# Last expert tile: down weights loaded and used in five equal-width steps, the last narrow piece issued from ScalarE's queue

## What is computed

```
h = silu(ragged_dot(xs, w_gate, sizes)) * ragged_dot(xs, w_up, sizes)     # 2048 -> 512 per expert
y = ragged_dot(h, w_down, sizes)                                          # 512 -> 2048
y = y * gates_flat[order][:, None]
out = zeros_like(xt).at[token_of].add(y)
h = h + out
return rms_norm(h, final_norm_g)
```

## Time and profile before

| | us |
|---|---|
| median of 3 runs | 1982.48 |
| lowest and highest | 1981.11, 1984.16 |
| the profiled execution, its own time | 1982.84 |
| its span in the trace | 1980.0 |
| mean granted TensorE clock | 0.954 |

### The profile page before, as it was taken

One profiled execution on the slowest core, in us unless ns is written; L12 is line 12 of the kernel. 1 busy time (PEld: TensorE's weight loads), 2 busy tenths in 40 slices (PEclk: granted clock), 3 DMA queues, 4 the chain that ended last, 5 costly groups with the idle time before them and its releaser, 6 DMA issues.

```text
span 1980.0 us, 30734 instructions
## 1 busy us (share of the span) xinstructions
PE 1791.9 (91%) x12867; PEld 1139.0 (58%) x12867; DVE 788.3 (40%) x1516; ACT 248.2 (13%) x580; POOL 178.8 (9%) x204
## 2 busy tenths in 40 slices
PE   6999999999999989999355899999999999999666
PEld 4888999789997879999311233333333333333222
DVE  7666595277467544333400122221222222223015
ACT  3012111200325331000200000000000000000004
POOL 1453342000000000000100000000000000000000
PEclk9999999999999999999677899999999999999888
DMA  5343333321222232221699999999999999999996
GB/s 216 109 130 92 90 104 87 98 65 43 65 70 75 70 146 86 65 85 44 289 423 421 425 425 422 423 423 422 418 422 412 420 423 426 417 423 423 408 405 225
DMA packets 80393, 506.58 MB, mean 256 GB/s; under 512 B 18785, under 2 KB 23029, under 8 KB 46977
## 3 DMA queue, kind: packets, MB, share of 16 engines
q1 hardware_dynamic: 62706, 480.40, 60.4%
q0 software_dynamic: 5152, 15.81, 2.4%
q10 hardware_dynamic: 12400, 8.36, 1.7%
HBM read 498.32 MB, written 12.99 MB: 258 GB/s over the span
## 4 chain that ended last, share of the span: by engine, by line
PE 71%; DMA 20%; DVE 4%; issue 2%; ACT 1%; SPq 1%; ACTq 0%; DVEq 0%; POOL 0%; POOLq 0%
PE psum L958 20%; PE psum L1269 17%; PE psum L961 15%; DMA arena<-in_moe_w_gate 14%; PE psum L1233 6%; PE psum L1296 3%; DMA arena<-in_moe_w_up 3%; DMA arena<-in_moe_w_down 3%; PE psum L1116 2%; DVE arena L1704 2%; PE psum L1017 1%; PE psum L1363 1%; PE psum L1375 1%; DVE arena L1707 1%; DMA arena<-hs_rows,arena 1%
## 5 line engine op out<-in xcount | busy, mean ns | idle before, releaser
L1269 PE MATMUL psum<-arena 128*32 128x512 f32 x3584 | 423.1, 627 | 82.4 <-DMA arena<-in_moe_w_gate 34.6
L958 PE MATMUL psum<-arena 128*128 128x128 f32 x3584 | 412.6, 277 | 3.5 <-issue 3.5
L958 PEld LDWEIGHTS psum<-arena 128*128 128x128 f32 x3584 | 407.0, 193 | 10.9 <-issue 10.4
L1704 DVE TENSOR_TENSOR arena<-psum,arena 128x512 f32<-128x512 f32 (+1 forms) x319 | 211.7, 680 | 402.1 <-PE psum L1233 379.5
L1269 PEld LDWEIGHTS psum<-arena 128*32 128x32 f32 x3584 | 120.4, 115 | 378.0 <-issue 376.9
L961 PE MATMUL psum<-arena 128*128 128x256 f32 x1456 | 322.4, 380 | 1.1 <-DVE arena L1704 1.1
L961 PEld LDWEIGHTS psum<-arena 128*128 128x128 f32 x1456 | 273.4, 190 | 39.0 <-issue 2.1
L1704 DVE TENSOR_TENSOR arena<-arena,psum 128x256 f32<-128x256 f32 (+2 forms) x172 | 75.1, 437 | 473.0 <-PE psum L958 217.1
L1296 PE MATMUL psum<-arena 128*32 128x512 f32 x1664 | 185.9, 605 | 20.9 <-DMA arena<-in_moe_w_down 20.6
L1704 DVE TENSOR_TENSOR arena<-arena 128x240 f32<-128x240 f32 (+17 forms) x464 | 187.4, 446 | 33.0 <-ACT arena L1424 25.2
L1233 PE MATMUL psum<-arena 128*128 128x512 f32 x416 | 192.4, 605 | 0.0
(11 more groups left out here) (213 smaller groups left out, 993.0 us busy)
## 6 DMA issues: line engine op xcount, KB each, us to landing
arena<-in_moe_w_gate SPq DMA_DIRECT2D x64, 2048.0 KB, 28.0
arena<-in_moe_w_up SPq DMA_DIRECT2D x64, 2048.0 KB, 26.3
arena<-in_moe_w_down SPq DMA_DIRECT2D x60, 2048.0 KB, 27.9
arena<-in_w_in SPq DMA_DIRECT2D x86, 512.0 KB, 4.6
arena<-in_w_out SPq DMA_DIRECT2D x32, 512.0 KB, 4.6
arena<-in_x SPq DMA_DIRECT2D x8, 1024.0 KB, 8.3
hs_rows<-arena ACTq DMA_DIRECT2D x4, 1024.0 KB, 4.8
arena<-in_moe_w_down SPq DMA_DIRECT2D x4, 1024.0 KB, 15.2
```

The lines of the kernel that those rows point to most:

```text
L958: last = mm(B(bank, [(1, P)], off=t * P), F(a + t * P, P), F(w + i * P, P), start=start and t == 0, stop=(i == KH - 1), skip_group_check=True)
L1269: last = mm(B(bank, [(1, FE)], 32 * g, 32), F(XT + c * CAP + 32 * g, 32), F(SLOT[slot] + (c % 8) * FE, FE), start=(c == 0), stop=(c == KD ...
L1704: return v.tensor_tensor(o, a, b, op)
```

## The change

Pieces 0 and 1 are loaded apart, each with one load per expert of 512 columns (1 MB, rows of 2 KB). SP issues pieces 0 to 3 in order. The four loads of piece 4 leave SP's queue: ACT issues two of them between its silu and its copy of the hidden activations, and two between its copies of the gain and its copy of piece 0. It waits on `slot_used` of buffers 4 to 7 for them, and loads the four expert numbers into registers beforehand. PE works all five pieces product by combination. DVE takes them in the same order, and does two of the four `times_g` of piece 3 behind its copy of piece 4.

```diff
-        PIECES = ((0, 512, 16, 0, D // 2), (512, 512, 16, 512, D // 2), (1024, 512, 20, 0, 512), (1536, 256, 20, D, 256),
+        PIECES = ((0, 512, 16, 0, 512), (512, 512, 16, D, 512), (1024, 512, 20, 0, 512), (1536, 256, 20, D, 256),
                   (1792, 256, 20, D + 1024, 256))
@@ SP
-            for k in range(4):
-                slot, n = parts[16 + k]
-                sp.wait_ge(slot_used[slot], n + 1)
-                sp.dma_start(V(SLOT[slot], [(D // 2, FT2), (1, D // 2)]),
-                             down_columns(four[k], 0, D // 2)).then_inc(slot_in[slot], 16)
...
+            for p, (lo, cols, first, at_, row) in enumerate(PIECES[:LASTP]):
                 for k in range(4):
+                    slot, n = parts[first + k]
+                    dst = V(SLOT[slot] + at_, [(row, FT2), (1, cols)])
+                    if at_ == 0:
+                        sp.wait_ge(slot_used[slot], n + 1)
+                        sp.dma_start(dst, down_columns(four[k], lo, cols)).then_inc(slot_in[slot], 16)
+                    else:
+                        sp.dma_start(dst, down_columns(four[k], lo, cols)).then_inc(tail_in[p], 16)
@@ PE
-                y_part(0)
-                y_part(1)
-                combine_part(0)
-                combine_part(1)
-                for p in range(2, NPC):
+                for p in range(NPC):
                     y_part(p)
                     combine_part(p)
@@ ACT
                 A(F(SIL, FE), B(2, [(1, FE)]), ACT.Silu).then_inc(silu_done, 1)
+                if between is not None:
+                    between()
                 act.wait_ge(hT_full, n + 2)
...
+            four = [act.value_load(ORDV[0:1, bass.ds(NE - 4 + k, 1)], min_val=0, max_val=NE - 1) for k in range(4)]
+
+            def last_columns(ks):
+                lo, cols, first, at_, row = PIECES[LASTP]
+                for k in ks:
+                    slot, before = last_parts()[first + k]
+                    act.wait_ge(slot_used[slot], before + 1)
+                    act.dma_start(V(SLOT[slot] + at_, [(row, FT2), (1, cols)]),
+                                  down_columns(four[k], lo, cols)).then_inc(tail_in[LASTP], 16)
+
+            hidden_act(LAST, ends(last_parts())[0], lambda: last_columns((0, 1)))
...
+            last_columns((2, 3))
             y_copy_last(0)
@@ DVE
-            y_copy(1)
             dve.wait_ge(fg_done, 4)
-            for p in (0, 1):
...
+            for p in range(LASTP):
+                if not Y_ACT[p]:
+                    y_copy(p)
                 for t in range(TB):
                     add(t, p)
-            for p in (0, 1):
...
+                if p < LASTP - 1:
+                    for t in range(TB):
+                        times_g(t, p)
+            times_g(0, LASTP - 1)
+            times_g(1, LASTP - 1)
             y_copy(LASTP)
+            times_g(2, LASTP - 1)
+            times_g(3, LASTP - 1)
```

More of the change, by code:

```diff
@@ L512, in build @@
         fg_in, fg_spread, fg_done = sem("fg_in"), sem("fg_spread"), sem("fg_done")
-        tail_in = [sem("tail_in0"), sem("tail_in1")]
+        tail_in = [None, sem("tail_in1"), None, sem("tail_in3"), sem("tail_in4")]
         g_done, out_dve, out_act, out_done = (
@@ L619, in build, with down_columns @@
         wg_d, wu_d, wd_d = d["moe_w_gate"], d["moe_w_up"], d["moe_w_down"]
+        def down_columns(e, lo, n):
+            return wd_d[bass.ds(e, 1), :, lo:lo + n].rearrange("e (m p) n -> p (e m) n", p=P)
         block = ctx.enter_context(nc.Block())
@@ L653, in part @@
                 sp.dma_start(dst, half_of_expert(e, which, half)).then_inc(slot_in[slot], 16)
-            def down_columns(e, lo, n):
-                return wd_d[bass.ds(e, 1), :, lo:lo + n].rearrange("e (m p) n -> p (e m) n", p=P)
             def expert(i):
@@ L701, in _ @@
                 part(four[j % 4], parts[j], j // 8, j // 4 % 2)
-            for k in range(4):
-                slot, n = parts[16 + k]
-                sp.wait_ge(slot_used[slot], n + 1)
-                sp.dma_start(V(SLOT[slot], [(D // 2, FT2), (1, D // 2)]),
-                             down_columns(four[k], 0, D // 2)).then_inc(slot_in[slot], 16)
[L707 to L712, removed]
-                for k in range(4):
-                    slot = parts[20 + k][0]
-                    sp.dma_start(V(SLOT[slot] + at_, [(row, FT2), (1, n)]),
-                                 down_columns(four[k], lo, n)).then_inc(tail_in[i], 16)
+            for p, (lo, cols, first, at_, row) in enumerate(PIECES[:LASTP]):
+                for k in range(4):
+                    slot, n = parts[first + k]
[5 more added lines that the diff above has]
+                        sp.dma_start(dst, down_columns(four[k], lo, cols)).then_inc(tail_in[p], 16)
             for t in range(TB):
@@ L1353, in y_part @@
                     here = parts[first:first + 4]
-                    if p >= 3:
-                        pe.wait_ge(tail_in[p - 3], 4 * 16)
-                    elif p != 1:
+                    if at_:
+                        pe.wait_ge(tail_in[p], 4 * 16)
+                    else:
                         for slot, before in here:
@@ L1604, in _, with hidden_act @@
             A(F(RE2, TB), F(RDF, TB), ACT.Exp).then_inc(gates_exp, 1)
-            def hidden_act(n, gate_end):
+            def hidden_act(n, gate_end, between=None):
                 slot, before = gate_end
@@ L1638, in _ @@
                 act.wait_ge(o_added, NOV * 16 + 17)
-            hidden_act(LAST, ends(last_parts())[0])
+            four = [act.value_load(ORDV[0:1, bass.ds(NE - 4 + k, 1)], min_val=0, max_val=NE - 1) for k in range(4)]
[7 more added lines that the diff above has]
+            hidden_act(LAST, ends(last_parts())[0], lambda: last_columns((0, 1)))
             for q in range(4):
```

## The result

| | median, us | runs | ratio to before (95% interval) |
|---|---|---|---|
| before | 1982.35 | 22 | |
| changed | 1985.95 (1983.13 to 1989.31) | 22 | 1.0018 (1.0012 to 1.0024) |

The change costs 3.6 us, 0.18%: clear of zero, and just inside the 0.2% that the prediction took as the line (the interval reaches beyond that line). The profiled execution has a span of 1985.2 us, 5.2 us longer than the one of before, and was itself one of the longer ones (1987.65 us).

The account below looks back on a forecast made before the run. The landing at 1932.2 and PE's chain behind it set the end. Piece 2 starting 2.2 us late was the only term: 1982.48 + 2.2 = 1984.7 us; range 1981.0 to 1988.0, the forecast's own 1983.9 to 1985.4.

Parts of the forecast that it names:

- The gain at piece 0: On PE, piece 0's product starts 2.7 us sooner; after exposed copies PE is ready for piece 2 0.7 us sooner.
- The landing of piece 2: Piece 4's early loads go ahead of piece 2, which lands at 1950.3; PE starts its product 2.2 us later.
- The price of sharing, by whole loads: On the DMA engines, piece 2 lands after 12 loads of 1 MB plus all of piece 4, 5.95 to 7.4 us.
- ACT held at its issue: Rival: each ACT issue of piece 4 waits up to 4.9 us for SP's; 1986.9 or 1991.4 us; chance 0.14.
- The clock in the new wait: Rival: PE's clock falls while waiting for piece 2, its product takes 3.4 us more; 1988.1 us; chance 0.08.
- DVE's new order and the four register loads: DVE's gain products stay hidden, reordering piece 3's costs at worst 0.1 us; ACT's register loads fall in idle time, costing nothing.

Follow-up runs that it names:

- the old cut: The kernel before, with ACT issuing piece 4's loads; pieces 0 and 1 stay one load of 4 KB rows per expert: 1984.96 us, ratio 1.0012.

## Why the prediction was right or wrong

**The gain at piece 0: right.** Expected: start 1929.6, end of the product 1934.9, of the combination 1939.4, ready for piece 2 at 1947.5, 0.7 us sooner than before. Measured: 1929.74, 1934.7, 1939.04 and 1947.2. The copies stand open in the chain at 0.71 and 0.81 us. The kernel without ACT's loads agrees with the sum, 1.2 us below against the 0.7 forecast, but its interval includes no gain at all.

**The landing of piece 2: right, to 0.2 us partly by luck.** Expected 1950.3 and a start at 1950.4, 2.2 us late; measured 1950.5 and 1950.63, 2.4 us late. The 1950.3 was the middle of a range with no reason for it (6.7 us for piece 4), on top of 1943.6 for the rest; with piece 4 last on SP the rest landed at 1944.3, and 6.2 us separate that from the changed kernel. The reason held, since the same order of bytes on one queue gave the same loss, and a late second queue gave none. By the Trainium skill's rule on queues ("DMA: Bandwidth & Descriptors", section "Queues, rings and completion order") the engines take turns by packet; 901 packets against 901 in the old cut's trace agree.

**The price of sharing, by whole loads: right for piece 2, too simple elsewhere.** The prediction charged piece 2 with all of piece 4. That is right, since all of piece 4 is through by 1942.2. The expectation for the old cut charged pieces 0 and 1 in the same way, and that was twice too much (2.1 us, not 4 to 5): only part of ACT's rows had their turn by then, which explains some of it, and the rest is open. Piece 1 landed in time in the changed kernel (PE took it at 1939.04 without a wait), so that nothing of the forecast hung on this.

**ACT held at its issue: a rival, refuted.** ACT's four issues took 0.38 to 0.42 us. The last two (0.94 us for both, from 1929.19) stand within an issue of SP's that lasted 7.22 us. First that SP issue, then ACT's last:

```profile
L708 SPq DMA_DIRECT2D arena<-in_moe_w_down x1: 7220/7220/7220, 1927.6 to 1927.6; - x1
...
L1638 ACTq DMA_DIRECT2D arena<-in_moe_w_down x1: 383/383/383, 1929.7 to 1929.7; - x1
```

Had ACT's issue had to wait for the end of SP's, it would have ended after 1934.8. The Trainium skill ("Perfetto Trace Analysis", section "DMA Instruction — HWDGE (DVE, Sync)") says that an issue holds a lock on the shared descriptor generator until its descriptors are made. In this trace SP cannot have held such a lock for the whole of its issue; what SP was waiting for in it, no run shows. The chance of 0.14 rested on this rival, and the upper part of the range on it and on the clock.

**The clock in the new wait: the step that was mis-sized.** The sum held nothing for it. It was put as a rival beside the forecast with a chance of 0.08 and a price of 3.4 us. Both traces of the changed kernel show it, at 2.8 and 1.3 us, on top of the late landing: it is a consequence of the wait, and belonged in the sum with the chance that the wait gives it. The price was that of a product done wholly at the low level; in both traces the clock came back before the end. The wait was also longer than the 2 to 3 us that the rival was weighed with (3.44), since PE came 0.3 us sooner and the data 0.2 us later. The result lies 1.25 us above the forecast and 0.55 us above the forecast's own range, though inside the whole one. The loss is 3.6 us where 2.2 was forecast, and the clock is the only term the runs show that is large enough for the difference; its exact part of the median is not shown.

**DVE's new order and the four register loads: nil, as expected.** The copy of piece 1 starts at 1942.75, with the products of the gain done at 1942.25 (DVE rows of after):

```profile
1939.76 2.49 DVE L1707 TENSOR_TENSOR arena<-arena 128x512 f32<-128x512 f32 x4
1942.75 0.69 DVE L2386 COPY arena<-psum 128x512 f32<-128x512 f32 x1 [0.50 <-PE psum L1357]
```

The half microsecond of idleness between them says that DVE waited for PE, not PE for DVE. The first add of piece 4 begins 0.8 us after PE's last combination starts, before and after the change (1963.97 in the earlier trace rows, the combination at 1963.17).

## What to carry to other kernels

A load on a second queue is not behind the first queue's backlog: it takes its turns at once, row for row. Give a second queue only what is needed next, or issue it late. When an edit opens a wait on PE, add to the wait's length the half-speed products that may follow it, and look first whether other PE work can be moved into idle time that is already there. Here that was worth 3.0 us on top of the finer cut, and only because of it: in the kernel before, the data of piece 0 came after the spread of the gain, so that by these rows an earlier spread alone had nothing to gain.

A probe that adds instructions can move more than the engine it fills. Compare the landings with and without it before the medians are read as one term.

## What the runs showed of the hardware

- Two DMA queues are served packet by packet: 901 to 901 packets in 8 us, with 0.90 against 2.13 MB. The smaller rows got the smaller share of the bytes.
- ACT's issue of a load was not held up by a long issue of SP's: 0.38 us within 7.22 us.
- SP's issues lengthen while another queue takes turns: the four of piece 2 took 16.88 us after the change and 10.18 us in the earlier trace rows. SP had nothing else to do, so it cost nothing here.
- With three to five products added on PE, loads that PE waits for landed some 1.5 us later: 17.0 to 17.1 us after the issue instead of 15.5 to 15.7, and 15.6 instead of 14.1 with the gain spread early. In each of these comparisons a 16 KB load of instructions, 1.05 us long, stood ahead of the landing with the added products and behind it without them; that it is the cause is not shown.
- The granted clock fell in empty waits of 3.44, 3.08 and 2.83 us and held in one of 2.75 us; once it fell 0.7 us behind a wait of 2.39 us.
